# SSD row sums from exact bf16 parts laid out in advance; decayed x and scaled state made by GpSimd, in a one-core decoder layer

## What is computed

```python
a_cs = jnp.cumsum(a, axis=-1)                       # a = dt * A, per head, within a chunk
Lmat = jnp.exp(segsum(a))                           # exp(a_cs[l] - a_cs[s]) for l >= s, else 0
CB = jnp.einsum('bclgn,bcsgn->bgcls', Cc, Bc)
y_diag = jnp.einsum('bgrcls,bcsgrp->bclgrp', CB[:, :, None] * Lmat, X)
decay = jnp.exp(a_cs[..., -1:] - a_cs)
states = jnp.einsum('bclgn,bgrcl,bclgrp->bcgrpn', Bc, decay, X)
... # state carried from chunk to chunk: state = exp(a_cs[-1]) * state + states
y_off = jnp.einsum('bclgn,bcgrpn,bgrcl->bclgrp', Cc, states_in, jnp.exp(a_cs))
```

## Time and profile before

| | before |
|---|---|
| median of 3 runs, us | 1031.6 (1030.83 to 1033.43) |
| profiled execution, us | 1030.6 |
| its span, us | 1028.8 |
| PE busy | 992.1 us, 96% |
| DVE busy | 653.3 us, 63% |
| ACT busy | 337.8 us, 33% |
| POOL busy | 185.2 us, 18% |
| granted TensorE clock, mean | 0.995 |

### The profile page before, as it was taken

One profiled execution on the slowest core, in us unless ns is written; L12 is line 12 of the kernel. 1 busy time (PEld: TensorE's weight loads), 2 busy tenths in 40 slices (PEclk: granted clock), 3 DMA queues, 4 the chain that ended last, 5 costly groups with the idle time before them and its releaser, 6 DMA issues.

```text
span 1028.8 us, 13941 instructions
## 1 busy us (share of the span) xinstructions
PE 992.1 (96%) x4467; PEld 559.9 (54%) x4468; DVE 653.3 (63%) x1642; ACT 337.8 (33%) x958; POOL 185.2 (18%) x220
## 2 busy tenths in 40 slices
PE   8999999999999989989998999999999999999997
PEld 4444475444545555667667875555664444444443
DVE  3331221444345788988754998755678888878884
ACT  3321122111124677877776753232110000000000
POOL 0030051110000130011100401011031333233333
PEclk8999999999999999999999999999999999999999
DMA  7301042012100200000002314233659888999332
GB/s 269 106 28 48 1 85 82 1 41 75 34 1 1 82 1 2 1 2 2 1 1 99 107 16 158 89 122 130 246 167 369 266 289 314 378 375 329 117 112 94
DMA packets 73689, 119.26 MB, mean 116 GB/s; under 512 B 13889, under 2 KB 53153, under 8 KB 73633
## 3 DMA queue, kind: packets, MB, share of 16 engines
q1 hardware_dynamic: 62544, 87.59, 25.3%
q0 software_dynamic: 11088, 30.95, 8.6%
HBM read 105.41 MB, written 21.50 MB: 123 GB/s over the span
## 4 chain that ended last, share of the span: by engine, by line
PE 47%; DVE 15%; ACT 5%; issue 2%; DMA 0%; POOL 0%; DVEq 0%; POOLq 0%; ACTq 0%
PE ps L1860 17%; PE ps L1870 8%; PE ps L2183 5%; PE ps L1154 3%; PE ps L1165 3%; PE ps L1224 3%; PE ps L1192 3%; ACT ring_gate_up L1263 2%; DVE ring_gate_up L1325 2%; ACT big_u L1272 2%; DVE misc L291 1%; PE ps L2214 1%; DVE ring_gate_up L2402 1%; DVE big_u L2402 1%; DVE ring_down L2524 1%
## 5 line engine op out<-in xcount | busy, mean ns | idle before, releaser
L1674 DVE STREAM_TRANSPOSE big_w<-big_w 32x256 f32<-32x256 f32 x384 | 167.4, 436 | 28.9 <-DMA big_w<-hn_dram,misc 22.4
L1860 PE MATMUL ps<-ring_gate_up,big_w 128*128 (+1 forms) x400 | 179.8, 592 | 0.3 <-ACT big_w L1914 0.3
L517 PE MATMUL ps<-big_w,big_u 128*128 128x512 f32 (+1 forms) x448 | 177.0, 550 | 1.0 <-DMA big_w<-in_w_in 1.0
L517 PEld LDWEIGHTS ps<-big_w,big_u 128*128 128x128 f32 x448 | 84.8, 194 | 79.0 <-issue 72.4
L1860 PEld LDWEIGHTS ps<-ring_gate_up,big_w 128*128 128x128 f32 x400 | 74.0, 190 | 83.8 <-issue 83.7
L1263 ACT ACTIVATE ring_gate_up<-ring_gate_up,big_w 128x64 f32<-128x64 f32 (+8 forms) x192 | 106.0, 561 | 1.1 <-DVE big_w L1325 1.1
L1870 PE MATMUL ps<-ring_down,big_w 128*128 x200 | 90.0, 593 | 0.6 <-ACT big_w L1904 0.6
L1272 ACT ACTIVATE big_u<-ps 128x512 f32<-128x512 f32 (+1 forms) x126 | 66.3, 584 | 72.4 <-PE ps L1165 72.4
L1165 PE MATMUL ps<-ident,ring_gate_up 128*128 128x128 f32 x488 | 66.0, 279 | 10.1 <-ACT ring_gate_up L1263 5.0
L1165 PEld LDWEIGHTS ps<-ident,ring_gate_up 128*128 128x128 f32 x488 | 52.7, 141 | 27.2 <-ACT ring_gate_up L1263 13.5
L1870 PEld LDWEIGHTS ps<-ring_down,big_w 128*128 128x128 f32 x200 | 37.9, 190 | 48.1 <-issue 48.1
(11 more groups left out here) (391 smaller groups left out, 1434.0 us busy)
## 6 DMA issues: line engine op xcount, KB each, us to landing
ring_gate_up<-in_w_gate SPq DMA_DIRECT2D x16, 1024.0 KB, 8.3
ring_gate_up<-in_w_up SPq DMA_DIRECT2D x16, 1024.0 KB, 11.8
ring_down<-in_w_down SPq DMA_DIRECT2D x16, 1024.0 KB, 13.7
misc<-in_x SPq DMA_DIRECT2D x16, 512.0 KB, 3.5
big_w<-in_w_in SPq DMA_DIRECT2D x6, 1024.0 KB, 7.1
big_w<-in_w_out SPq DMA_DIRECT2D x8, 512.0 KB, 5.0
hn_dram<-big_u SPq DMA_DIRECT2D x8, 512.0 KB, 2.6
out<-ring_gate_up SPq DMA_DIRECT2D x8, 512.0 KB, 3.7
```

Of the source, the lines that this page charges most:

```text
L517: last = nc.tensor.matmul(ps[:, b, 0:width], uT[:, k, c * P:(c + 1) * P], wbuf[:, n % 2, k, 0:width], start=(k == 0), stop=(k == KD - 1))
L1674: last = nc.vector.transpose(dst[j * 32:(j + 1) * 32, :, i * 32:(i + 1) * 32], src[i * 32:(i + 1) * 32, :, j * 32:(j + 1) * 32])
L1860: last = nc.tensor.matmul(ps[:, 2 + b, :], xT[:, b, k, :], ring_gu[:, bass.ds(at + k * 2 * D_EXP, BANK)], start=(k == 0), stop=(k == KD - 1))
```

## The change

Three things.

1. The cumulative sums are also made once with tokens along the free axis: one more product in `ssd_constants`, whose 64 x 128 result DVE splits into three bf16 parts. DVE also makes a small 0/1 table, `chunk_hot`. SP stores the parts to DRAM and loads them back as `sum_rows` (24 partitions x 1024, bf16). In `operands`, per group, the 4 float32 products of L1522 become one bf16 product of 512 columns over 24 rows.
2. POOL makes x_decay and `kept` = state times its decay. DVE's L1619 and L1649 go; before L1651 DVE waits for `state_kept`, and for c = 0 it takes `state` itself. PE waits for `x_decayed` ahead of L1551. POOL's last four weight blocks are scaled one at a time in iterations c = 2 to 5, between x_decay and `kept`.
3. `kept` and the parts lie in `ffn_rows`, so SP loads the norm row later: after `y_ready` and x's second tile, ahead of expert 0.

```diff
--- before.py
+++ after.py
@@ -208,6 +208,12 @@
     M["misc"] = sb("misc", [P, 3 * 1024])
     M["ones"] = sb("ones", [P, P])[:, :]
     M["ffn_rows"] = sb("ffn_rows", [P, D])[:, :]
+    M["sum_rows"] = M["ffn_rows"][0:3 * NT, 0:512].bitcast(BF16)
+    M["sum_parts"] = M["ffn_rows"][0:NT * SH, 512:704].bitcast(BF16).rearrange("m (t q) -> m t q", t=3)
+    M["sum_rest"] = M["ffn_rows"][0:NT * SH, 704:704 + P]
+    M["chunk_hot"] = M["small"][0:3 * NT, 496:500].bitcast(BF16)
+    M["sum_rows_dram"] = nc.dram_tensor("sum_rows_dram", (3 * NT, SH * P), BF16, kind="Internal").ap()
+    M["s_sum_rows"] = N.sem("sum_rows_stored_then_loaded")
     M["ps"] = N.ps("ps", [P, 8, BANK])
     M["s_w_out"] = [N.sem("w_out_loaded0"), N.sem("w_out_loaded1")]
     M["dt_steps"] = N.sem("dt_steps")
@@ -1125,6 +1131,11 @@
         sp.wait_ge(z_copied, NT - Z_HEAD)
         for k in range(KD // 2, KD):
             sp.dma_start(M["big_w"][:, k * D:(k + 1) * D], A["w_out"][0, k * P:(k + 1) * P, :]).then_inc(M["s_w_out"][1], 16)
+        sp.wait_ge(dt_sem, 8)
+        sp.dma_start(M["sum_rows_dram"].rearrange("(t c) (h q) -> (c h) t q", t=3, q=P), M["sum_parts"])\
+            .then_inc(M["s_sum_rows"], 16)
+        sp.wait_ge(M["s_sum_rows"], 16)
+        sp.dma_start(M["sum_rows"], M["sum_rows_dram"]).then_inc(M["s_sum_rows"], 16)
 
     def tensor(pe):
         def transpose_bank(use):
@@ -1214,7 +1225,8 @@
             pe.wait_ge(dt_sem, 6)
             bank = transpose_bank(prep_use)
             nc.tensor.matmul(ps[:, bank, 0:64], tri[:, :], flat(1), start=True, stop=True)
-            nc.tensor.matmul(ps[:, bank, 64:128], ones, flat(1), start=True, stop=True).then_inc(prep_full, 1)
+            nc.tensor.matmul(ps[:, bank, 64:128], ones, flat(1), start=True, stop=True)
+            nc.tensor.matmul(ps[0:NT * SH, bank, 128:128 + P], flat(1), tri[:, :], start=True, stop=True).then_inc(prep_full, 1)
 
         def z_pieces(a, b):
             for i in range(a, b):
@@ -1393,7 +1405,16 @@
             dve.wait_ge(prep_full, 1)
             prep.mark(nc.vector.tensor_scalar(flat(2), ps[:, bank, 0:64], -1.0, None, ALU.mult))
             prep.mark(nc.vector.tensor_copy(flat(4), ps[:, bank, 0:64]))
-            prep.done(nc.vector.tensor_copy(flat(5), ps[:, bank, 64:128]))
+            prep.mark(nc.vector.tensor_copy(flat(5), ps[:, bank, 64:128]))
+            sums, parts, rest = ps[0:NT * SH, bank, 128:128 + P], M["sum_parts"], M["sum_rest"]
+            prep.done(nc.vector.tensor_copy(parts[:, 0, :], sums))
+            prep.done(nc.vector.tensor_tensor(rest, sums, parts[:, 0, :], ALU.subtract))
+            prep.done(nc.vector.tensor_copy(parts[:, 1, :], rest))
+            prep.done(nc.vector.tensor_tensor(rest, rest, parts[:, 1, :], ALU.subtract))
+            prep.mark(nc.vector.tensor_copy(parts[:, 2, :], rest))
+            pair = M["small"][0:3 * NT, 500:508]
+            prep.done(nc.vector.tensor_tensor(pair, ident[0:3 * NT, 0:NT], ident[0:3 * NT, NT:2 * NT], ALU.add))
+            prep.done(nc.vector.tensor_tensor(M["chunk_hot"], pair, ident[0:3 * NT, 2 * NT:3 * NT], ALU.add))
             nc.vector.tensor_tensor(flat(3), flat(5), flat(4), ALU.subtract).then_inc(dt_sem, 1)
             dve.wait_ge(dt_sem, 7)
             nc.vector.tensor_copy(flat(6)[:, 0:1], flat(3)[:, 0:1]).then_inc(dt_sem, 1)
@@ -1456,6 +1477,7 @@
     decT = u[:, 5120:7168].rearrange("p (b h l) -> p b h l", b=2, h=SH)
     b_nat = u[:, 7168:7680].rearrange("p (b g n) -> p b g n", b=2, g=NG)
     state = u[:, 7680:8192].rearrange("p (h d) -> p h d", h=SH)
+    kept = M["ffn_rows"][:, 512:1024].rearrange("p (h d) -> p h d", h=SH)
     y = M["misc"][:, 0:1024].rearrange("p (b h d) -> p b h d", b=2, h=SH)
     ones = M["ones"]
     junk = M["misc"][:, 2048:2048 + 256]
@@ -1474,9 +1496,10 @@
     x_read, b_read, cb_read, dec_read = sem("x_natural_read"), sem("b_natural_read"), sem("cb_read"), sem("decay_read")
     y_full, y_read = sem("y_full"), sem("y_read")
     st_full, st_ready = sem("new_states_full"), sem("state_ready")
+    x_decayed, state_kept = sem("x_decayed"), sem("state_kept")
     y_ready = sem("y_ready")
     ready = SsdReady(x_read, b_read, cb_read, dec_read, y_read, y_ready)
-    ord_dve, ord_act, in_steps = sem("vector_order3"), sem("scalar_order3"), sem("first_chunk_steps")
+    ord_dve, ord_act = sem("vector_order3"), sem("scalar_order3")
     set_up, z_ready = sem("ssd_set_up"), sem("z_silu_done")
     X_BANK, CB_BANK, DEC_BANK, YD_BANK, YO_BANK, ST_BANK = 0, 1, 2, 4, 5, 6
 
@@ -1488,14 +1511,26 @@
         pool.wait_ge(AT.z_copied, AT.z_tiles)
         nc.gpsimd.memset(u[:, 7680:8192], 0.0).then_inc(set_up, 1)
 
-        for k in [*range(KD // 2, KD), *range(KD // 2)]:
-            if k == 0:
-                attention_tables(pool)
+        def scale_weights(k):
             if k % 4 == 0:
                 pool.wait_ge(M["s_w_out"][k // 4], 16 * KD // 2)
             wk = M["big_w"][:, k * D:(k + 1) * D]
             nc.gpsimd.tensor_scalar(wk, wk, M["vecT"][:, M["V_AON"] + k:M["V_AON"] + k + 1], None, ALU.mult)\
                 .then_inc(M["w_out_scaled"], 1)
+
+        for k in range(KD // 2, KD):
+            scale_weights(k)
+        attention_tables(pool)
+        for c in range(NT - 1):
+            pool.wait_ge(x_read, c + 1)
+            if c >= 2:
+                pool.wait_ge(st_full, c - 1)
+            nc.gpsimd.tensor_tensor(x_decay[:, c % 2], x_dt[:, c % 2], heads(decay[:, c, :]), ALU.mult).then_inc(x_decayed, 1)
+            if 2 <= c < 2 + KD // 2:
+                scale_weights(c - 2)
+            if c >= 1:
+                pool.wait_ge(st_ready, c)
+                nc.gpsimd.tensor_tensor(kept, state, heads(e_tot[:, c, :]), ALU.mult).then_inc(state_kept, 1)
 
     def operands(pe, c):
         tok = slice(3 + c * P, 3 + (c + 1) * P)
@@ -1518,10 +1553,10 @@
             o = ps[:, DEC_BANK + g, :]
             nc.tensor.matmul(o, identb[:, :], M["masksb"][:, :].unsqueeze(1).broadcast_to([P, GQ, P]),
                              start=True, stop=True, skip_group_check=True)
-            for r in range(GQ):
-                last = nc.tensor.matmul(o[:, r * P:(r + 1) * P],
-                                        a[:, c, g * GQ + r:g * GQ + r + 1].broadcast_to([P, P]), tri[:, :],
-                                        start=False, stop=True, skip_group_check=True)
+            if c == 0:
+                pe.wait_ge(M["s_sum_rows"], 32)
+            last = nc.tensor.matmul(o, M["chunk_hot"][:, c:c + 1].broadcast_to([3 * NT, P]),
+                                    M["sum_rows"][:, g * BANK:(g + 1) * BANK], start=False, stop=True, skip_group_check=True)
         last.then_inc(pre_full, 1)
 
     def tensor(pe, AT, first_tile):
@@ -1547,6 +1582,7 @@
             if c == 0:
                 pe.wait_ge(AT.rows_done, 1)
             if c + 1 < NT:
+                pe.wait_ge(x_decayed, c + 1)
                 for g in range(NG):
                     last = nc.tensor.matmul(ps[:, ST_BANK, g * GW:(g + 1) * GW], b_nat[:, c % 2, g, :],
                                             x_decay[:, c % 2, g * GQ:(g + 1) * GQ, :], start=True, stop=True)
@@ -1606,17 +1642,15 @@
     def heads(v):
         return v.unsqueeze(2).broadcast_to([P, v.shape[1], HD])
 
-    def chunk_in(dve, o, c):
+    def chunk_in(dve, c):
         dve.wait_ge(pre_full, c + 1)
         b = c % 2
         if c >= 2:
             dve.wait_ge(y_full, c - 1)
             dve.wait_ge(st_full, c - 1)
         xs = ps[:, X_BANK, :].rearrange("p (h d) -> p h d", h=SH)
-        o.mark(nc.vector.tensor_tensor(x_dt[:, b], xs, heads(dt[:, c, :]), ALU.mult))
+        nc.vector.tensor_tensor(x_dt[:, b], xs, heads(dt[:, c, :]), ALU.mult)
         nc.vector.tensor_tensor(x_skip[:, b], xs, heads(M["head_rows"][:, 2, :]), ALU.mult).then_inc(x_read, 1)
-        o.wait()
-        o.done(nc.vector.tensor_tensor(x_decay[:, b], x_dt[:, b], heads(decay[:, c, :]), ALU.mult))
         dve.wait_ge(b_read, c + 1)
         for g in range(NG):
             dve.wait_ge(dec_read, NG * c + g + 1)
@@ -1627,7 +1661,7 @@
     def first_vector(dve):
         dve.wait_ge(prep_done, 3)
         dve.wait_ge(set_up, 1)
-        chunk_in(dve, Order(dve, in_steps), 0)
+        chunk_in(dve, 0)
 
     def vector(dve, next_transposes):
         o = Order(dve, ord_dve)
@@ -1646,9 +1680,10 @@
             dve.sem_inc(y_read, 1)
             if c + 1 < NT:
 
-                o.done(nc.vector.tensor_tensor(state, state, heads(e_tot[:, c, :]), ALU.mult))
+                if c >= 1:
+                    dve.wait_ge(state_kept, c)
                 dve.wait_ge(st_full, c + 1)
-                nc.vector.tensor_tensor(state, state, ps[:, ST_BANK, :].rearrange("p (h d) -> p h d", h=SH),
+                nc.vector.tensor_tensor(state, kept if c >= 1 else state, ps[:, ST_BANK, :].rearrange("p (h d) -> p h d", h=SH),
                                         ALU.add).then_inc(st_ready, 1)
             if c >= 1:
```

(5 more changed lines are left out.)

## The result

| us | before | changed |
|---|---|---|
| median beside the first measurement | 1031.47 (1030.83 to 1033.43, 4 runs) | 1024.43 (1024.16 to 1026.49, 4 runs) |
| profiled execution | 1030.6 | 1024.16 |
| its span | 1028.8 | 1022.4 |
| PE busy | 992.1 | 984.1 |
| DVE busy | 653.3 | 647.3 |

The ratio is 0.9938 (95% interval 0.9925 to 0.9950): faster by 0.5 to 0.75%. The same kernel was measured twice more, beside other runs of the kernel before: 0.9964 (0.9941 to 0.9986; median 1028.73 of 7) and 0.9938 (0.9916 to 0.9961; median 1025.55 of 5). Over all 16 runs its median is 1025.7, and that of the kernel before 1031.4 over the 47 runs beside the experiments: 5.7 us, less than the first 7.0.

A forecast was written before the change was run, and what follows sets the result against it. DVE was taken to set SSD's pace, PE just behind. SSD's -9.1 us and the constants' +1.8 gave -7.3, from 1030.6 to 1023.3, or 1024 as a median; range 1019.5 to 1028.5.

The forecast's parts named there:

- `kept` collides in every chunk: Rival: POOL's `kept` meets DVE's L1657 in three more chunks, +2.7 us, 1026 (1027 as a median); chance 0.17.
- What bounds it: In SSD's steady chunk DVE sets the pace at 7.33 us, and PE follows 0.26 us below it.
- DVE's chunk, 5.88: Steady SSD chunk on DVE: without L1619 and L1649 it falls by 1.45, from 7.33 to 5.88 us.
- The collision: POOL's `kept` meeting DVE's L1657: 0.9 us each (bounds 0 and 1.27), in c = 2 and c = 6, +1.8.
- There it costs nothing: In c = 3 to 5 POOL starts `kept` only after L1657 has started; L1654 meets the block 1.9 us in.
- A reading of the earlier trace: DVE's L1649 and L1657 beside POOL weight blocks: hindered, ending 0.97 us after block start; blocks hinder only in their first microsecond.
- The full lock: Rival: POOL's block holds L1654, then `kept` takes L1657, c = 3 to 5: +5.7, 1029; chance 0.11, shared with dear product.
- The new product: PE, `operands`: the bf16 product takes 0.21 us for 0.89 a group, saving 1.36 a chunk; PE's chunk 5.71.
- ACT in chunk 6: ACT's 7.40 us for chunk 5 makes DVE wait some 0.45 us in chunk 6, which gains 1.0.
- POOL's round: x_decay, weight block and `kept` on POOL take 5.4 us a chunk, under 5.9, delaying neither PE nor DVE.
- The constants: Seven added DVE instructions in attention, before PE's scores near 442 us: +1.8 us in full, bounds 0 and 2.1.
- The norm row: SP's later load of the norm row, 3.29 us to issue, ahead of expert 0 and x's third tile: costs nothing.

The follow-up runs named there:

- The products alone: Only the bf16 products with parts, store and reload; DVE makes x_decay and scales the state as in the kernel before. 1031.61 us, ratio 0.9994 against that kernel.
- the kernel with 128 rows: The changed kernel with the new bf16 product over 128 rows, 104 of them zero, instead of 24. One run, 1027.16 us.

## Why the prediction was right, and where its steps were off

The time was right to half a us (1024 for 1024.43), and partly by luck: the sum said -7.3, the trace shows -5.0 for the change itself, and the rest of the first difference was clock in unchanged code. Over all runs the difference is 5.7. At the clock of the kernel before, the profiled execution would be 1030.6 - 5.0 = 1025.6 us: the forecast's sum gave 1023.3, and its rival "`kept` collides in every chunk" 1026.0. That rival, with a chance of 0.17, is also what the rows show. Its time lies inside the stated range as well, so the time alone didn't decide between the two.

- **What bounds it: right.** DVE sets the pace and PE follows closely. The products alone, with DVE untouched, left the steady chunk at 7.33.
- **DVE's chunk, 5.88: right** as a floor. It is 5.95 without the collision: L1686 now waits for L1678 directly, so the cut of L1649 saves 0.65 and not 0.73.
- **The collision: mechanism and price right, place wrong.** 0.76 us for 0.9. The step that failed is "There it costs nothing", for c = 3 to 5. It rested on x_decay at 1.27 us from the earlier trace rows; with a broadcast second input it takes 1.04, so `kept` started 0.14 us ahead of L1692 instead of just behind it. The trace of the kernel before had such operations: its L1119, with a broadcast second input, takes 1.26 us for 640 columns. I had the order of two starts hang on 0.25 us and called it settled. It cost about 0.8 us a chunk in three chunks.
- **A reading of the earlier trace rows: wrong.** The prediction has L1649 and L1657 both end 0.97 us after their block's start. The blocks began at 571.15 and 573.98 and the two operations ended at 572.81 and 575.65, which is 1.7 us later; what lies about 0.97 us behind the block's start is where the last 0.69 us of each begin. That a block hinders in its first us stands.
- **The full lock: didn't come, as forecast.** By the Trainium skill ("SBUF — State Buffer", section "SBUF: two separate sides") the pair is held for the whole instruction. For the two-input operations the traces agree: 1.45 and 1.57 for 0.69 on DVE, 1.55 for 1.04 on POOL, according to who began first. For a weight block they don't: L1689 at 576.85, with two SBUF inputs and 2.2 us into a block, took 0.68 in each of the three chunks with a block. The two hindered rows don't either: they were let go about 1 us into a block of 2.84.
- **The new product: mis-sized.** 0.31 for 0.21, and the mask product as much, +0.41 a chunk on PE. PE's own chunk is 5.98 and not 5.71: 0.24 less, since it was 6.83 before and not 7.07, 0.42 more for the products and 0.10 more for the product behind them (0.97 us to its successor for 0.87). In a steady chunk it was hidden. At the entry, where PE is on the path, chunk 2's second L1657 came at 567.35 instead of 566.6, 0.8 us late (timeline, DVE). Twice 0.41 would be that; the kernel with 128 rows confirms 0.3 for the first of the two chunks.

```profile
567.35 0.69 DVE L1657 TENSOR_TENSOR big_u<-big_u,ps 128x512 f32<-128x512 f32 x1 [0.27 <-ACT big_u L1615]
```

- **ACT in chunk 6: right in kind**, but hidden by the collisions. Without them it costs 1.2 (0.45 forecast).
- **POOL's round: right.** No DVE row waits for POOL.
- **The constants: right.** +1.6 for +1.8, on the path in full, as the kernels with and without the steps show.
- **The norm row: right.** It was issued at 617.14 and nothing waited for it.

SSD by chunks, from one second L1657 to the next (the first line from SSD's first transpose), against the kernel before:

| up to | forecast, us | measured, us | what made the difference |
|---|---|---|---|
| chunk 2 | -3.0 | -2.2 | the new product |
| chunk 3 | -1.7 | -1.8 | |
| chunk 4 | -1.45 | -0.6 | collision |
| chunk 5 | -1.45 | -0.6 | collision |
| chunk 6 | -1.0 | -0.6 | collision, where 0.45 of waiting for ACT was forecast |
| chunk 7 | -0.5 | -0.7 | |
| sum | -9.1 | -6.6 | |

## What to carry to other kernels

When work moves from VectorE to GpSimd, look at what VectorE does at the moment it releases GpSimd: if its next operations have two SBUF inputs, they can meet. Release GpSimd one semaphore later, behind them, when its result has time; here that one wait was worth 2.5 us on top of SSD's 6.6. A part of a change that relieves an engine just behind the bound shows nothing in the steady chunk by itself (the products alone: 7.33 as before); it pays once the other engine is faster. A step of a prologue that only one engine can begin (here the copy out of PSUM) need not be finished by that engine. And when two starts lie within a few tenths of a us, neither order is a forecast: price both.

## What the runs showed of the hardware

- An operation of GpSimd with two inputs, 128x512 float32, took 1.04 us when the second input was broadcast along the free axis, and 1.27 when it was not the earlier trace rows.
- Operations of VectorE and GpSimd with two SBUF inputs each that meet take turns: the second one is longer by most of what is left of the first (VectorE 1.45 for 0.69 when GpSimd began 0.14 us ahead, 1.57 when 0.02 ahead; GpSimd 1.55 for 1.04 when VectorE began 0.05 ahead). GpSimd's product of 1024 columns with one value per partition hindered VectorE only in its first us.
- A bf16 product of 512 columns is followed by the next after 0.21 us when both have 128 rows, and after 0.31 when the rows change from 128 to 24 or back.
- The granted clock fell to half (1.2 of 2.4 GHz), for 3 to 10 us at a time, in places that differed between executions of one kernel: at 284, 346, 452, 552, 570, 574 and 740 us in various profiles. Ahead of many falls PE had idled (2.4 of 4 us busy before the one at 574; 2 us of waiting at the entry), but the same idleness stood in profiles where the clock stayed up, and ahead of the fall at 284 PE's rows are busy without a gap from 264 us on. One such fall cost 1.6 us in the input projection. The times of one kernel spread over up to 8 us, and the mean clock explains this only in part: the kernel before took 1034.42 us at 0.998 and 1028.66 us at 0.996. When the falls come, and what else spreads the times, is open.
